# A two-layer decoder on one core: modulation chunks laid out by a table, summed from one accumulator

## The reference, cut to what matters

```python
D_MODEL, SEQ, DEPTH, HEAD_DIM = 2048, 256, 2, 128
c_act = silu(c)
for l in range(2):
    mod = c_act @ w_mod[l] + b_mod[l]            # 3 * 2048 numbers
    shift, scale, gate = split(mod, 3)
    h = rmsnorm(x, norm_gain[l]) * (1 + scale) + shift
    proj = h @ w_in[l]                           # 2048 x 7504
    ...                                          # sparse attention, 8 heads; retention, 8 heads
    y = concatenate([y_a, y_b]) @ w_out[l]       # 2048 x 2048
    x = x + gate * y
...                                              # second block: five more projections, hgrn, conv
```

## Time and profile before

| | us |
|---|---|
| median of 3 executions (lowest, highest) | 1975.12 (1973.83, 1976.34) |
| the profiled execution | 1976.41 |
| its span, first to last instruction | 1974.5 |
| TensorE matmuls busy | 1895.3 |
| VectorE busy | 1352.1 |
| ScalarE busy | 967.2 |
| GpSimd busy | 327.5 |

### The profile page before, as it was taken

The page is one execution under the profiler, slowest core; times in us unless marked ns, Lnnn a source line. Parts: engine busy times, 40 slices in busy tenths (PEclk is TensorE's granted clock), DMA queues, the critical chain, the costliest instruction groups (busy, mean ns, idle before and its releaser), DMA issues.

```text
span 1974.5 us, 24792 instructions
## 1 busy us (share of the span) xinstructions
PE 1895.3 (96%) x9184; PEld 1580.9 (80%) x9184; DVE 1352.1 (68%) x1937; ACT 967.2 (49%) x1307; POOL 327.5 (17%) x395
## 2 busy tenths in 40 slices
PE   4989999989898999999999999999999999999995
PEld 4878788778786887888878888888888888878884
DVE  8989989776598986755566544487875456665544
ACT  5454455344534444555454644466664445443643
POOL 0000002073113000206411000044431020030000
PEclk9999999999998999999999999999999999999998
DMA  9979968765496995554455555554445555556551
GB/s 351 356 252 354 330 215 280 250 228 160 160 338 228 320 349 183 193 167 155 141 175 192 188 192 192 192 171 152 156 160 171 192 192 172 192 177 215 187 171 64
DMA packets 210769, 420.09 MB, mean 213 GB/s; under 512 B 7137, under 2 KB 12013, under 8 KB 209773
## 3 DMA queue, kind: packets, MB, share of 16 engines
q1 hardware_dynamic: 209004, 413.08, 62.0%
q10 hardware_dynamic: 1664, 5.66, 0.8%
HBM read 416.59 MB, written 2.11 MB: 212 GB/s over the span
## 4 chain that ended last, share of the span: by engine, by line
PE 93%; DVE 4%; ACT 1%; issue 1%; POOL 0%; DMA 0%; DVEq 0%; ACTq 0%; POOLq 0%
PE acc L559 27%; PE acc L561 27%; PE acc L560 27%; PE tps L657 2%; PE sps L864 1%; DVE scr L1617 1%; PE sps L683 1%; DVE w_lo L1494 1%; PE tps L608 1%; PE tps L529 1%; PE acc L683 0%; PE tps L707 0%; DVE proj L1589 0%; DVE proj L1617 0%; PE tps L810 0%
## 5 line engine op out<-in xcount | busy, mean ns | idle before, releaser
L1494 DVE TENSOR_TENSOR w_lo<-raw,w_hi 128x1024 fp32r<-128x1024 f32 (+1 forms) x596 | 757.4, 1278 | 523.3 <-ACT w_hi L1043 510.3
L1043 ACT ACTIVATE w_hi<-raw 128x1024 fp32r<-128x1024 f32 (+1 forms) x596 | 623.8, 1051 | 794.5 <-PE acc L561 674.0
L559 PE MATMUL acc<-w_hi,ht_hi 128*128 128x512 f32 (+1 forms) x2384 | 948.3, 398 | 9.9 <-DVE w_lo L1494 5.1
L561 PE MATMUL acc<-w_hi,ht_lo 128*128 128x512 f32 (+1 forms) x2384 | 930.4, 390 | 0.0
L560 PE MATMUL acc<-w_lo,ht_hi 128*128 128x512 f32 (+1 forms) x2384 | 928.9, 390 | 0.0
L559 PEld LDWEIGHTS acc<-w_hi,ht_hi 128*128 128x128 f32 x2384 | 451.5, 189 | 101.0 <-issue 13.5
L561 PEld LDWEIGHTS acc<-w_hi,ht_lo 128*128 128x128 f32 x2384 | 450.5, 189 | 94.4
L560 PEld LDWEIGHTS acc<-w_lo,ht_hi 128*128 128x128 f32 x2384 | 451.9, 190 | 86.9
L1617 DVE SCALAR_TENSOR_TENSOR scr<-raw,vcol,scr 128x512 f32<-128x512 f32 x280 | 198.2, 749 | 7.2 <-DMA raw<-in_w_mod 0.3
L2209 POOL TENSOR_TENSOR scr<-scr 128x128 f32<-128x128 f32 x56 | 31.0, 585 | 157.6 <-DVE scr L1944 157.6
L657 PEld LDWEIGHTS tps<-kst,scr 128*128 128x128 f32 x320 | 51.4, 248 | 2.1 <-DVE scr L1617 1.1
(11 more groups left out here) (258 smaller groups left out, 1411.4 us busy)
## 6 DMA issues: line engine op xcount, KB each, us to landing
raw<-in_w_in SPq DMA_DIRECT2D x208, 1024.0 KB, 5.1
raw<-in_w_mod SPq DMA_DIRECT2D x96, 1024.0 KB, 6.7
raw<-in_w_out SPq DMA_DIRECT2D x32, 1024.0 KB, 5.1
raw<-in_w_o SPq DMA_DIRECT2D x16, 1024.0 KB, 5.1
raw<-in_w_ple_gate SPq DMA_DIRECT2D x16, 1024.0 KB, 5.1
raw<-in_w_b_out SPq DMA_DIRECT2D x8, 1024.0 KB, 5.2
raw<-in_w_a_out SPq DMA_DIRECT2D x8, 1024.0 KB, 5.1
raw<-in_w_in SPq DMA_DIRECT2D x8, 672.0 KB, 4.2
```

Source lines behind the costliest of these rows:

```text
L559: pe.matmul(o, hi_m, w_hi[:, slot, u, 0:width], start=start, stop=False)
L561: mm = pe.matmul(o, lo_m, w_hi[:, slot, u, 0:width], start=False, stop=stop)
L1043: act.activation(w_hi[:, x % SPL, :, 0:width], raw[:, j, 2 * (x % halves):2 * (x % halves) + 2, 0:width], ACT.Copy).then_inc(hi_ready, 1)
L1494: dve.tensor_tensor(w_lo[:, x % SPL, :, 0:width], raw[:, j, 2 * (x % halves):2 * (x % halves) + 2, 0:width], w_hi[:, x % SPL, :, 0:width]. ...
```

## The change

A table replaces MODS. PIECES gives, for every weight chunk, the halves after which a quarter of a modulation chunk stands; FULL is (1, 3, 5, 7). From it `slots_of_chunks` works out PLAN: which slot of `raw` each transfer lands in, and which quarter of which modulation chunk follows which half. SyncE, ScalarE and VectorE all read it.

- In layer 0 the four modulation chunks of chunks 8 to 11 are spread over chunks 8 to 13: three quarters in each of 8 to 11 (halves 1, 3, 7), one in chunk 12 (half 7), three in chunk 13 (halves 1, 3, 5). They still come in order, so a modulation chunk now crosses chunk borders. All others stay where they were.
- After the last quarter VectorE adds the odd accumulator into the even one (one more instruction, 128x512, here called the fold; new line 1650) and signals `mod_ready`; `mod_sums` then makes four matmuls instead of eight. The eight modulation chunks before layer 0 keep both accumulators and eight matmuls.
- The sums of the four moved ones stand after half 1 of chunk 10, half 1 of chunk 11, half 3 of chunk 12 and half 5 of chunk 14; the takes at half 5, 5, 7 and 7. Before the first two TensorE waits for `qt_ready`, since the transposed q lies in the same bank. The retention of chunk 12 waits for the take before its transposes after half 6.
- The outputs of the last two heads move from half 1 to half 0 of chunk 12, in both layers.
- Loops of two turns in layer 0 are written out (chunks 8 to 11 and 15 to 18), as each turn now differs; the evacuations stand where they did.

```diff
...
-MODS = [(1, 2, 3, 4, 5, 8, 9, 10, 11, 16, 17, 18), (1, 2, 3, 4)]
+FULL = (1, 3, 5, 7)
+PIECES = [{1: FULL, 2: FULL, 3: FULL, 4: FULL, 5: FULL, 8: (1, 3, 7), 9: (1, 3, 7), 10: (1, 3, 7), 11: (1, 3, 7),
+           12: (7,), 13: (1, 3, 5), 16: FULL, 17: FULL, 18: FULL}, {1: FULL, 2: FULL, 3: FULL, 4: FULL}]
...
-        def pair_mods(l, k):
-            return tuple(tuple(c for c in (0, 1) if k + 2 * t + c in MODS[l]) for t in range(2))
+        def slots_of_chunks():
+            plan, item, piece = [{}, {}], 0, 4 * 8
+            for l in range(DEPTH):
+                for k in range(NCH + 5):
+                    rows, mods = [], {}
+                    for j in range(4):
+                        rows.append(item % RAW)
+                        item += 1
+                        if 2 * j + 1 in PIECES[l].get(k, ()):
+                            mods[2 * j + 1] = piece // 4, piece % 4, item % RAW
+                            item, piece = item + 1, piece + 1
+                    plan[l][k] = rows, mods
+                assert item % RAW == 0 and piece % 4 == 0
+            return plan
+        PLAN = slots_of_chunks()
+        SUM_AT, TAKE_AT = {}, {}
+        for l in range(DEPTH):
+            for k in range(NCH + 5):
+                for x, (n, q, slot) in PLAN[l][k][1].items():
+                    if q == 3:
+                        SUM_AT[n], TAKE_AT[n] = (l, k, 7), (l, k + 1, 3)
+                        if 8 <= k < 11:
+                            SUM_AT[n], TAKE_AT[n] = (l, k + 1, 1), (l, k + 1, 5)
+                        if k == 11:
+                            SUM_AT[n], TAKE_AT[n] = (l, 12, 3), (l, 12, 7)
+                        if k == 13:
+                            SUM_AT[n], TAKE_AT[n] = (l, 14, 5), (l, 14, 7)
+        SUMS, TAKES = ({v: n for n, v in d.items()} for d in (SUM_AT, TAKE_AT))
+        def home(n):
+            return macc_h if 8 + 5 <= n < 8 + 8 else macc
...
-            def with_mod(src, col, mod, mod_col):
-                for j in range(4):
-                    for n, (w, at) in enumerate(((src, col), (mod, mod_col))):
-                        slot = (2 * j + n) % RAW
-                        sp.wait_ge(raw_read, free.next(2))
-                        sp.dma_start(raw[:, slot, :, :], w(j, at, CH)).then_inc(raw_landed[slot], 16)
...
+                    rows, mods = PLAN[l][k]
+                    w, width = full(wi[l] if k <= NCH else wo[l]), TAIL if g == NCH else CH
+                    for j in range(4):
+                        land(rows[j], w(j, g * CH, width), width)
+                        if 2 * j + 1 in mods:
+                            n, q, slot = mods[2 * j + 1]
+                            land(slot, full(wm[n // 12])(q, n % 12 * CH, CH))
...
-                        if x // 8 in own_mods and x % 8 == 7 and late is None:
-                            pe.wait_ge(raw_read, lo.next(2))
-                            mod_sums(macc, n_mod % 2)
-                        elif x // 8 in own_mods and x % 2:
-                            lo.skip(2)
-                        if late is not None and x % 8 == 3 and (x // 8 - 1 in own_mods or (x < 8 and not first and mods[0])):
-                            mod_sums(late, (n_mod - 1) % 2)
+                        if at:
+                            l, k = at[0], at[1] + x // 8
+                            if x % 8 in PLAN[l][k][1]:
+                                lo.skip(2)
+                            if (l, k, x % 8) in SUMS:
+                                n = SUMS[l, k, x % 8]
+                                if 8 <= k < 12:
+                                    pe.wait_ge(qt_ready, qtr.ahead(2))
+                                mod_sums(home(n), n % 2)
...
+            def mod_sums(src, b, parts=1):
                 pe.wait_ge(mod_taken, m_taken.next())
+                if parts == 1:
+                    pe.wait_ge(mod_ready, m_ready.next())
                 for j in range(4):
-                    for e in range(2):
+                    for e in range(parts):
                         mm = pe.matmul(tps[:, 1, j:j + 1], src[:, b, e, j * P:(j + 1) * P], ones,
-                                       start=e == 0, stop=e == 1)
+                                       start=e == 0, stop=e == parts - 1)
                 mm.then_inc(mod_summed, 1)
...
-                if u == 0:
+                if u == 0 or u == 6:
...
-                gemm(2, chunk_halves(2), 8, mods=pair_mods(l, 8), late=macc_h, side=heads,
-                     side_per={a: 4 for a in (qn, qtr, prb, ptr, yr)}, drain=False)
...
+                    gemm(1, chunk_halves(2), 8, at=(l, 8), side=heads, drain=False)
+                    gemm(1, chunk_halves(2), 8, at=(l, 10), side=lambda t, x, first: heads(1, x, False), drain=False)
...
-                        if x % 8 == take_at and (x // 8 - 1 in own_mods or (x < 8 and (left if first else 1 in mods[0]))):
-                            mod_take(n_mod - 1)
-                        if x // 8 in own_mods and x % 2:
-                            mod_piece(macc if late is None else late, n_mod % 2, x % 8 // 2, j + 1)
+                        if at and here in TAKES:
+                            mod_take(TAKES[here])
+                        if at and x % 8 in mods:
+                            n, q, slot = mods[x % 8]
+                            mod_piece(home(n), n % 2, q, slot, one_sum=True)
...
+                if q == 3 and one_sum:
+                    dve.wait_ge(raw_read, own.ahead(0))
+                    dve.tensor_tensor(to[:, b, 0, :], to[:, b, 0, :], to[:, b, 1, :], ALU.add).then_inc(mod_ready, 1)
...
-                    if x == 0 and l == 0:
-                        mod_take(mod_at[0] - 1)
-                        mod_left[0] = False
-                    if x == 1:
+                    if x == 0:
                         outputs(GA + 2 * HD)
...
```

More of the change, by code:

```diff
@@ L530, in turn_pair @@
                         tr.then_inc(turned, 1)
-                assert turns <= 2 or not mods[1]
-                m_base = mod_n[0]
+                assert turns == 1 or not at
                 def body(t, first):
-                    own_mods, m0 = (mods[0], m_base) if first else (mods[1], m_base + len(mods[0]))
                     for x, (slot, kts) in enumerate(halves):
@@ L586, in gemm @@
                         body(i, False)
-                mod_n[0] += len(mods[0]) + (turns - 1) * len(mods[1])
-                if late is not None and mods[0]:
-                    pe.wait_ge(raw_read, lo.ahead(0))
-                    mod_sums(late, (mod_n[0] - 1) % 2)
-            mod_n = [8]
             def chunk_halves(n):
@@ L1032, in body @@
                 def body(t, first):
-                    own_mods = mods[0] if first else mods[1]
                     for x in range(nh):
                         j = x // halves % RAW
-                        if x // 8 in own_mods:
-                            j = 2 * j % RAW
-                            if x % halves == 0:
-                                landed[j + 1].skip(16)
+                        if at:
+                            rows, mods = PLAN[at[0]][at[1] + x // 8]
+                            j = rows[x % 8 // 2]
                         if x % halves == 0:
@@ L1062, in split @@
                     per = {slot_free: nh, results: nh if evac else 0, **(side_per or {})}
-                    per.update({s: 16 * nh // (RAW * halves) + 16 * len(mods[1]) for s in landed})
+                    per.update({s: 16 * nh // (RAW * halves) for s in landed})
                     with loop(act, turns - 1, per) as i:
@@ L1480, in take @@
                     evac(g, b)
-                assert turns <= 2 or not mods[1]
-                m_base, take_at = mod_at[0], 3 if late is None else 4
-                left = mod_left[0]
                 def body(t, first):
-                    own_mods, m0 = (mods[0], m_base) if first else (mods[1], m_base + len(mods[0]))
                     for x in range(nh):
                         j = x // halves % RAW
-                        n_mod = m0 + sum(c < x // 8 for c in own_mods)
-                        if x // 8 in own_mods:
-                            j = 2 * j % RAW
+                        if at:
+                            here = at[0], at[1] + x // 8, x % 8
+                            rows, mods = PLAN[here[0]][here[1]]
+                            j = rows[x % 8 // 2]
                         dve.wait_ge(hi_ready, hi.next())
@@ L1521, in split @@
                         per.update(owners[evac])
-                    per.update({s: 16 * nh // (RAW * halves) + 16 * len(mods[1]) for s in m_land})
-                    per[own] = nh + 8 * len(mods[1])
-                    if mods[1]:
-                        per.update({m_free: len(mods[1]), m_sum: len(mods[1])})
+                    per.update({s: 16 * nh // (RAW * halves) for s in m_land})
+                    per[own] = nh
                     with loop(dve, turns - 1, per) as i:
```

117 lines of the change are left out of this document (61 added, 56 removed).

## The result

| | before | after |
|---|---|---|
| median of 4 executions, us | 1974.83 | 1961.63 |
| lowest, highest | 1973.83, 1976.34 | 1958.36, 1962.82 |
| ratio, 95% interval | | 0.993 [0.9913, 0.9947] |
| the profiled execution, its span | 1976.41, 1974.5 | 1960.76, 1959.0 |

What follows compares the result with a forecast made beforehand. The prediction took TensorE, busy 96% of 1974.5 us, as the bound. Its terms, -16.3 - 12.6 + 2.5 + 0.5 = -25.9 us, gave a forecast of 1949.5 us, with a range of 1945 to 1957.

Steps and rivals of the forecast that it cites:

- Chunks 16 to 18 give their part back: Layer 0, chunks 16 to 18: VectorE paces TensorE, two halved sums not gained and 0.8 us lost, +2.5 us.
- rival 4: Ends of chunks: the fold comes late for the sum behind it, TensorE waits and the clock falls; 2000 us, chance 0.02.
- Stalls of heads: Layer 0, chunks 9 to 11: waits for late logits and the lower clock after them all go, -16.3 us.
- the line for chunks 8 to 14: Layer 0, chunks 8 to 14: stalls, four sums and qt together, forecast at -19.2 us.
- Rival 1: Chunks 9 to 11: logits stay late in part, TensorE stalls again; one chunk 1954 us, all three 1963; chance 0.15.
- Half the matmuls: Four matmuls instead of eight in each sum, 0.84 us less, over the fifteen on the path: -12.6 us.
- Rival 3: All sums: a sum costs a fixed time and doesn't halve, so 12.6 us are missing: 1961 us, chance 0.03.
- The fold: VectorE's add of the two accumulators, 0.69 us each, 16 times, hidden where VectorE has slack: 0.
- rival 2: VectorE paces chunks 16 to 18 harder, a fold stretched by 2.2 us twice: 1954 us, chance 0.07.
- Transfers: Weight transfers keep pace with the shorter chunks; full chunks need 368 GB/s; taken as 0, bounded at 1 us.
- qt waits: Sums of chunks 10 and 11 first wait for ScalarE's copies of q, 0.25 us each: +0.5 us, from 0 to 1.
- The wait before layer 1: TensorE idles 5.38 us on POOL before its first transpose, last sum and take beside it: 0, up to 1.5 us.

Runs made afterwards that it cites:

- the run of two sums: The changed kernel without the wait before chunk 17, with the fold taken out and both accumulators summed by TensorE again: 1961.7 us.

## Why the prediction was wrong

**The step that failed** is "Chunks 16 to 18 give their part back", and its premise, from the section on the change, that the written-out loops differ in their turns alone. VectorE's pace was computed in detail there, to +2.5 us, and was right: 81.47 us against 81.2 by the term, once the wait is out. What was not looked at is what each *call* does ahead of its first half. The order of instructions doesn't show it, since a wait is no row there, and the lines of the diff printed above leave these calls out; the arguments of the four calls do. The wait was in no term of the sum. It cost 7.8 us in the changed kernel's trace, 6.8 by the medians against the kernel before, and 8.8 in the kernel before. No rival had it: rival 4, the slower one, was a wait for VectorE at a chunk's end too, but for the fold, and none of the sixteen sums waits for its fold in the trace.

**Stalls of heads, -16.3**: right in cause, 0.6 us too large. A sum of 16 records costs 1.84 us with the restart of the matmuls behind it (chunk 10 against chunk 9 in the run of two sums, 27.47 against 25.63), not 1.68; so four sums are 7.4 of the 23.0 us and the stalls 15.6. That the line for chunks 8 to 14, with chunk 13 put right, meets the -19.2 to a tenth is luck in part: the half us forecast for qt wasn't spent. The waits of VectorE were read too broadly as well: 24.5 of the 33.3 us stood at the heads. The cause given, a late sum *and* a quarter at half 5, holds: two runs show that either one alone leaves TensorE almost without a wait. What was missed is chunk 13. I counted the quarters moved there for the transfers only, not for VectorE: 2.3 us, most of the 2.4 by which the line for chunks 8 to 14 falls short. Rival 1 had the mechanism (VectorE late by its quarters beside POOL), two chunks too early and for another operand.

**Half the matmuls, -12.6**: right where TensorE paces, 0.89 a sum with the restart of the matmuls behind it, so 13.3. Rival 3 is out.

**The fold, 0**: 15 of 16 take 0.69 us, as assumed, one 1.12 us, beside POOL. The Trainium skill, "GPSIMD Engine Reference", section "1. Specifications", has GpSimd's SBUF interfaces contend with VectorE's instructions of two SBUF inputs; by that rule the trace agrees for this one and for the quarter of 4.51 us in chunk 13. In chunks 17 and 18, where rival 2 put it, it took 0.69. But its cost was not 0 everywhere: in chunks 16 to 18 the folds took back more than the shorter sums brought (81.47 us with them, 80.82 with neither). Chunks 1 to 5 brought 3.2, not 4.2, and the loss is in chunk 4, which is 0.4 longer, not 0.8 shorter. Two things are changed there and weren't separated: w_hi of chunk 3 waits longer for its transfer (3.60 us against 2.76), the bound of 1 us under *Transfers*; and VectorE, with the fold, is busy 27.84 of the chunk's 29.18 us. The 5.21 us for a pair of halves left out the index's sums, 1.58 us a pair in chunk 4.

**qt waits, +0.5**: too much. Chunks 10 and 11 are 0.95 us longer than chunk 9, 0.81 for the sum and 0.14 for starting again; nothing for the copies. **Outputs one half earlier**: 0 in layer 1 (that chunk takes 26.38 us in both). **The wait before layer 1**, 0: right. TensorE is there 0.89 us earlier by its halved sum and waits that much longer, 6.27 us against 5.38:

```profile
611.56 0.66 PE L557 MATMUL tps<-kst,xn 128*128 128x128 f32 x2 [6.27 <-POOL xn L2134]
```

**The range** had no room for an unlooked-for wait of 8 us. Rival 1 reached to 1963 and rival 3 stood at 1961, but the heads don't stall and the sum did halve: neither is the reason.

## What to carry to other kernels

When a loop is written out into several calls, list for each call what it does before its body: waits, drains, default arguments. A full drain costs least where the evacuation it waits for comes first on its engine: here 2.2 us, not 7.8. Work moved from the pacing engine to another pays by the stretch: in chunks 16 to 18, where both engines are nearly full, 0.69 us more on VectorE for each sum took back all that the shorter sums would have brought. And before spreading work to cure a stall, test whether its order alone is enough; here a sum two halves earlier did it all.

## What was not expected of the hardware

The clock did not follow the length of a wait alone. In the changed kernel TensorE idled from 549.13, and the granted clock was 0.50 from 551.4 to 561.6. In the run with the evacuation moved, 1.76 us of waiting behind a sum were followed by 0.62 over 4.40 us and a first matmul of 0.77 us. In chunk 13 of the changed kernel, 2.29 us of waiting left it at 1.00:

```profile
454.50:456.80 2.30, 0.04 (x1) 0.00 (x0) 2.30 (x5) 0.00 (x0) 0.00 (x0) 1.00 1.07 342
456.80:474.17 17.37, 17.34 (x88) 14.75 (x89) 13.68 (x30) 6.60 (x12) 0.00 (x0) 1.00 0.70 215
```

What tells these apart stays open. So does the spread of some 3 us between executions of one kernel, of which chunk 4 (27.89 to 30.18 us with nothing changed before it) is a part.
